# Front of a diffusion-step kernel: who sums the squares, when the roots are taken, and where the position rows and two coefficient pieces stand

## What is computed

```python
xs = x_sample + _grid_pos_embed(rows, GRID_W, D_MODEL)      # latent tokens, tiles 0 to 7; tile 8 is context
mod = silu(c) @ ada_w + ada_b                               # 1024 x 6144: shift, scale, gate, twice
h = x * rsqrt(mean(x * x) + eps) * norm1_g * (1 + sc1) + sh1
z = h @ w_in                                                # 1024 x 1280
```

## Time and profile before

| | |
|---|---|
| median of 3 runs | 1289.15 us (1288.95 to 1290.19) |
| profiled execution, its own time | 1290.97 us |
| its span, first to last instruction | 1289.2 us |
| mean granted PE clock over the span | 0.971 |
| busy: PE, DVE, ACT, POOL | 94%, 66%, 40%, 42% |

### The profile page before, as it was taken

One profiled execution on the slowest core, in us unless ns is written; L12 is line 12 of the kernel. 1 busy time (PEld: TensorE's weight loads), 2 busy tenths in 40 slices (PEclk: granted clock), 3 DMA queues, 4 the chain that ended last, 5 costly groups with the idle time before them and its releaser, 6 DMA issues.

```text
span 1289.2 us, 21127 instructions
## 1 busy us (share of the span) xinstructions
PE 1207.0 (94%) x7402; PEld 1057.2 (82%) x7402; DVE 854.6 (66%) x1329; ACT 513.7 (40%) x915; POOL 540.4 (42%) x375
## 2 busy tenths in 40 slices
PE   6879899975899998999999999999999999999996
PEld 2469788965457888899999999999889999999995
DVE  6459599899744266776677676677855555555558
ACT  3673711254255557433333334333332344243223
POOL 3589444662331005453554444554423333333330
PEclk9889999988899999999999999999899999999998
DMA  8915355878932425656666666765676777777781
GB/s 309 383 51 169 93 176 163 104 168 217 382 139 98 131 75 210 222 200 209 240 231 213 212 207 200 245 231 208 205 252 243 256 268 268 251 246 262 251 279 72
DMA packets 189649, 268.65 MB, mean 208 GB/s; under 512 B 14046, under 2 KB 108552, under 8 KB 186904
## 3 DMA queue, kind: packets, MB, share of 16 engines
q1 hardware_dynamic: 188128, 262.67, 62.0%
q0 software_dynamic: 1280, 4.72, 0.9%
q10 hardware_dynamic: 184, 0.55, 0.2%
HBM read 186.62 MB, written 81.26 MB: 208 GB/s over the span
## 4 chain that ended last, share of the span: by engine, by line
PE 78%; POOL 7%; issue 3%; DVE 3%; DMA 3%; ACT 3%; SPq 2%; DVEq 0%; POOLq 0%; ACTq 0%
PE banks L934 23%; PE banks L936 22%; PE banks L935 22%; PE banks L1213 3%; DMA ad<-in_ada_w 2%; PE banks L970 1%; PE banks L1093 1%; POOL wct L750 1%; POOL wct L748 1%; POOL sst L863 1%; PE banks L1110 1%; POOL wct L743 1%; PE banks L1116 1%; POOL wct_tmp L746 1%; POOL wct_tmp L744 1%
## 5 line engine op out<-in xcount | busy, mean ns | idle before, releaser
L886 POOL TENSOR_TENSOR raw13r<-raw13s,w13h 128x512 fp32r<-128x512 f32 x110 | 155.0, 1418 | 467.3 <-ACT w13h L1710 443.9
L935 PE MATMUL banks<-ntr,w13h 128*128 128x256 f32 (+1 forms) x1144 | 337.2, 295 | 0.0
L934 PE MATMUL banks<-ntr,w13h 128*128 128x256 f32 (+1 forms) x968 | 283.7, 293 | 3.2 <-POOL raw13r L886 2.1
L935 PEld LDWEIGHTS banks<-ntr,w13h 128*128 128x128 f32 x1144 | 216.5, 189 | 0.9
L934 PEld LDWEIGHTS banks<-ntr,w13h 128*128 128x128 f32 x968 | 183.5, 190 | 5.4 <-issue 2.3
L934 PE MATMUL banks<-f2h,f_hi 128*128 128x512 f32 x396 | 156.6, 396 | 0.4 <-DVE acc L2419 0.4
L936 PE MATMUL banks<-f2h,f_lo 128*128 128x512 f32 x396 | 156.3, 395 | 0.0
L935 PE MATMUL banks<-f2l,f_hi 128*128 128x512 f32 x396 | 156.2, 395 | 0.0
L936 PE MATMUL banks<-ntr,raw13r 128*128 128x256 f32 (+1 forms) x528 | 153.7, 291 | 0.0
L2285 DVE TENSOR_TENSOR acc<-acc,banks 128x512 f32<-128x512 f32 x170 | 112.8, 683 | 39.0 <-PE banks L936 30.8
L890 POOL TENSOR_TENSOR f2l<-f2s,f2h 128x1024 fp32r<-128x1024 f32 x44 | 106.1, 2433 | 34.6 <-ACT f2h L1714 34.6
(11 more groups left out here) (328 smaller groups left out, 2527.0 us busy)
## 6 DMA issues: line engine op xcount, KB each, us to landing
raw13s<-in_ffn_w SPq DMA_DIRECT2D x66, 512.0 KB, 4.5
parts<-w13h SPq DMA_DIRECT2D x110, 256.0 KB, 2.5
w13h<-parts SPq DMA_DIRECT2D x110, 256.0 KB, 2.7
f2s<-in_ffn_w SPq DMA_DIRECT2D x44, 512.0 KB, 4.2
ad<-in_ada_w SPq DMA_DIRECT2D x20, 1024.0 KB, 10.6
parts<-wsumr SPq DMA_DIRECT2D x66, 256.0 KB, 2.6
wsumr<-parts SPq DMA_DIRECT2D x55, 256.0 KB, 4.9
parts<-raw13r SPq DMA_DIRECT2D x44, 256.0 KB, 2.9
```

The lines of the kernel that those rows point to most:

```text
L886: nc.gpsimd.tensor_tensor(w13_low(x, f), w13_low(x, f, F32), w13h[x][:, :, :].bitcast(F32), ALU.subtract).then_inc(sem("w13_lo"), 1)
L934: nc.tensor.matmul(out, hi_w, hi_x, start=start, stop=False)
L935: nc.tensor.matmul(out, hi_w, lo_x, start=False, stop=False)
```

## The change

Tile sums 5 to 8 move from ACT to DVE, as `tensor_tensor_reduce` with an accumulator output; the product itself is thrown into the place where the scaled tile will stand later. DVE makes sum 5 after the last step of group 0, then the position adds 6 and 7, the inverse of group 1, sums 6, 7 and 8, and the inverse of group 2. ACT takes group 2's root behind the second step of group 1. PE makes position row 2 behind the raw transposes, rows 3, 4 and 5 in front of the modulation tiles 3, 4 and 5 instead of behind them, and rows 6 and 7 behind block 0 instead of inside it, in other banks. POOL makes coefficient piece 1 directly behind piece 0, issues the transfers of both behind the column halves 3 to 5, and makes the low part of weight tile 1 behind the column halves 6 and 7.

```diff
+    POS_BANK = (5, 6, 7, 5, 6, 7, 7, 6)
+    POS_PRIOR = (None, None, None, 0, 1, 2, 5, 4)
+    SQ_ACT = 5
...
         wc_piece(0)
+        wc_piece(1)
         w_low(0)
         for i in range(3, 6):
             pos_add(i)
-        w_low(1)
+        pool.wait_ge(sem("gsc"), 1)
+        wc_out(0)
+        wc_out(1)
         pos_add(6)
         pos_add(7)
-        pool.wait_ge(sem("gsc"), 1)
-        wc_out(0)
+        w_low(1)
         x_scale(3)
-        wc_piece(1)
-        wc_out(1)
         for i in range(6, 9):
             x_scale(i)
...
             if i >= 3:
-                pe.wait_ge(sem("pos_half"), i - 2)
-            mm(B[5 + i % 3][:, :], row_sel[:, i, :], pos_r[:, :], start=True, stop=True).then_inc(sem("pos_bank"), 1)
+                pe.wait_ge(sem("pos_half"), POS_PRIOR[i] + 1)
+            mm(B[POS_BANK[i]][:, :], row_sel[:, i, :], pos_r[:, :], start=True, stop=True).then_inc(sem("pos_bank"), 1)
...
-        for i in range(3):
-            pos_row(i)
+        pos_row(0)
+        pos_row(1)
         raws_turn()
+        pos_row(2)
         pe.wait_ge(sem("polar"), 2)
-        for k in range(KT - 1):
-            ada_tiles(0, k, k + 1, B[4])
-            if k in (3, 4, 5):
-                pos_row(k)
+        ada_tiles(0, 0, 3, B[4])
+        pos_row(3)
+        ada_tiles(0, 3, 4, B[4])
+        pos_row(4)
+        ada_tiles(0, 4, 5, B[4])
+        pos_row(5)
+        ada_tiles(0, 5, 7, B[4])
         x_turns(0, 2)
...
             if s == 1:
-                pe.wait_ge(sem("pos_half"), 8)
+                pe.wait_ge(sem("pos_half"), 4)
...
-        z_with_turns(0, {1: 6, 3: 7})
+        z_with_turns(0)
+        pos_row(6)
+        pos_row(7)
         z_block(1)
...
-        for i in range(3, 6):
+        for i in range(3, 5):
             square_sum(i)
         root(1)
         z_out(0)
-        for n in range(KT, KT + 4):
+        for n in range(KT, KT + 2):
             h_out(n)
+        root(2)
+        act.sem_inc(sem("squares"), NT - SQ_ACT)
         z_out(1)
-        for n in range(KT + 4, 16):
+        for n in range(KT + 2, 16):
             h_out(n)
-        for i in range(6, 9):
-            square_sum(i)
-        root(2)
         w_high(2)
...
-            dve.wait_ge(sem("squares"), i1)
+            dve.wait_ge(sem("squares"), min(i1, SQ_ACT))
...
+        def square_sum(i):
+
+            if i < 8:
+                dve.wait_ge(sem("pos_half"), i + 1)
+                dve.wait_ge(sem("pos_cols"), i + 1)
+            else:
+                dve.wait_ge(sem("x8_in"), 16)
+            x = xt[i][:, :].rearrange("p (k n) -> p k n", n=P)
+            step(nc.vector.tensor_tensor_reduce(x_scaled(i), x, x, 1.0, 0.0, ALU.mult, ALU.add, accum_out=ss[:, i:i + 1]))
...
-            if n in (1, 3, 5, 7):
+            if n in (1, 3):
                 pos_add(4 + n // 2)
             if n == KT - 1:
+                square_sum(5)
+                pos_add(6)
+                pos_add(7)
                 dve.wait_ge(sem("pos_half"), 8)
                 inverse_ms(1)
+                for i in range(6, 9):
+                    square_sum(i)
+                inverse_ms(2)
             if n == 2 * KT - 1:
-                inverse_ms(2)
                 w_low(2)
```

More of the change, by code:

```diff
@@ L1032, in _, with z_with_turns @@
         x_turns(2, 3)
-        def z_with_turns(s, pos=()):
+        def z_with_turns(s):
             i, b = ZSEQ[s]
@@ L1046, in z_with_turns @@
                     x_turns(KT * b + k + 3, KT * b + k + 4)
-                if k in pos:
-                    pos_row(pos[k])
                 pe.wait_ge(sem("h_split"), KT * b + k + 1)
@@ L1952, in pos_add @@
             dve.wait_ge(sem(f"x{i}_in"), 16)
-            TT(xt[i][:, 0:512], xt[i][:, 0:512], B[5 + i % 3][:, :], ALU.add).then_inc(sem("pos_half"), 1)
+            TT(xt[i][:, 0:512], xt[i][:, 0:512], B[POS_BANK[i]][:, :], ALU.add).then_inc(sem("pos_half"), 1)
         def inverse_ms(g):
```

## The result

The changed kernel takes 1282.01 us (median of 5, 1278.08 to 1282.40) beside 1289.15 us: ratio 0.9933, interval 0.9915 to 0.9951. The forecast was 1285.9; the gain is 7.1 us where 3.3 were forecast, beyond the forecast's own range (1284.2 to 1287.7), inside the wide one (1281.0 to 1290.5), and at the time of the rival "L1978 gets its turn after one POOL operation" (1282.2). The profiled execution took 1278.08 us with a span of 1276.3, the shortest of the five, so its trace shows more gain than the median. Lines have moved: L1977 and L1978 of before are now L1993 and L1994, DVE's low parts L2000, the sums L1977. (L1993 is a subtraction in the code; this text goes on calling the two the first and the second addition.)

The account below looks back on a forecast made before the run. Two PE holes, before group 2's transposes and before `state_inputs`, were taken to hang on group 2's root. Group 2 -0.6 and the second hole -2.7 gave -3.3 from 1289.15: 1285.9 us; own range 1284.2 to 1287.7, wide 1281.0 to 1290.5.

Parts of the forecast that it names:

- L1978 gets its turn after one POOL operation: Rival, DVE's second addition near 34 us: it waits for one POOL operation, not a whole piece; 1282.2 us, chance 0.2.
- forecast -2.7: PE's hole before `state_inputs` at 140 us closes because pieces 2 to 7 start earlier: -2.7 us.
- the rival of half rate: Rival, accumulating sums on DVE: they run at half throughput, 1.3 us more each; 1289.4 us, chance 0.13.
- piece 1 is ready meanwhile, takes the port at 34.05 and, as at 101.36, keeps it to 41.6: DVE/POOL port at 34 us: POOL's piece holds up DVE's second addition to about 42.6; +2.6 us on group 0.
- 39.99 + 2.6: Start of group 0's first transposes: 39.99 us before the change, delayed 2.6 us by the held second addition.
- -0.6 for group 2's first split: DVE's first split of group 2, behind low part 2: 83.3 instead of 83.85, so -0.6 us for all behind it.
- the 7.11 us: Earlier trace, DVE's low part at 101.36: it lasted past four POOL operation boundaries, taken as waiting for a whole piece.
- forecast to 83.3: End of low part 2 on DVE, because piece 2 was to hold the port from 74.7 to 82.2.
- little reached PE: DVE's low part at 101.36 meeting the pieces: it cost 6 us of DVE; low parts 3 and 4 given one us either way.
- as the rival had it: Rival, group 1: the granted clock falls while PE waits from 66 to 70 us; 1292 us, chance 0.1.
- the shift passes to the end: Behind 140 us each stage reads what this one makes, so a shift there reaches the end in full.
- Rows at -1.2: Position rows 6 and 7 leaving block 0, where ACT waited 1.19 us at 54.74: -1.2 us.

Follow-up runs that it names:

- e3: Changed kernel with sums 5 to 8 and the roots back as before, on ACT; 1288.55 us, ratio 0.9991.
- e15: The kernel of e10 run once more (sums, early root and POOL wait alone); 1287.63 us, ratio 0.9978.
- e8: Changed kernel with POOL making low part 1 ahead of the four transfers and column halves 6 and 7; 1281.40 us, ratio 0.9942.
- e1: Changed kernel with DVE waiting for its own first addition before issuing the second; 1280.88 us, ratio 0.9938.
- e11: The changed kernel run once more, unaltered, for one profile; 1280.26 us (one execution).
- e9: The kernel of e5 with low part 2 also waiting for the fifth operation of piece 2; 1283.44 us, ratio 0.9954.
- e5: Changed kernel with DVE's second addition made to wait for the fifth operation of piece 1; 1284.02 us, ratio 0.9954.
- e2: Changed kernel with POOL's old order: piece 1 behind the scaling of tile 3, no early piece; 1286.07 us, ratio 0.9976.
- e6: The kernel of e2 with POOL waiting for its own four scalings in front of piece 2; 1282.02 us, ratio 0.9947.
- e10: Kernel before the change with only the sums, group 2's early root and POOL's wait before piece 2; 1287.28 us, ratio 0.9970.
- e14: The kernel of e10 with position rows 6 and 7, their banks and adds moved behind block 0; 1284.12 us, ratio 0.9964.
- e4: Changed kernel with the position rows in their old places and banks; 1280.94 us, ratio 0.9932.
- e13: The kernel of e4 with POOL waiting for its own four scalings before piece 2; 1279.63 us, ratio 0.9932.

## Why the prediction missed

**Right.** With the sums on DVE and group 2's root early, both holes close: 5.30 us at 82 us, 2.67 us at 140 us (forecast -2.7); without them (e3) both are there, 5.29 and 2.54 us. The second hangs on the pieces too: in e15, with the root early and piece 1 late, it is still 2.61 us. The sums cost 1.23 + 0.08 = 1.31 us each where they do not meet POOL, below the 1.5 taken; the rival of half rate (2.6 us and more) did not happen. The Trainium skill (Vector Engine (DVE) Microarchitecture Reference, Points that are easy to get wrong) has half throughput for an instruction that it calls S2S2D2_STT, with two non-bf16 SBUF sources; that would be, by an estimate, twice the 1.285 us of the earlier trace rows. The trace agrees with no halving here, 1.23 us, but it records the sums as CUSTOM_DVE_ANT_0, and no run shows whether the rule is meant for that form. Low part 1's later place cost nothing that e8 could show.

**The step that failed** is "piece 1 is ready meanwhile, takes the port at 34.05 and, as at 101.36, keeps it to 41.6". In the changed kernel's trace DVE went first; where POOL did (e1, e8, e11), DVE had its turn one operation later. The addition was over between 34.84 and 36.34 and not at 42.6, and group 0 waited for PE's own work alone: it started at 37.88, in e11 at 39.81, where 39.99 + 2.6 was forecast. The forecast's -0.6 for group 2's first split (83.85 to 83.3) became -6.02 (77.83; -4.71 in e11, 79.14); in the first trace another 1.1 us were won between it and the first `state_inputs` (135.77 before, 128.66 now), and with the hole of 2.67 this makes 9.8 of the landmark's 9.97; the medians show 7.1.

The step was taken from one row, the 7.11 us. The same trace had another, for DVE's low part of weight tile 2, which began while POOL was in its three scalings:

```profile
76.38 1.94 DVE L1984 TENSOR_TENSOR w_lo<-wst,w_hi 128x1024 fp32r<-128x1024 f32 x1 [1.35 <-ACT w_hi L1434]
```

It had the port behind the first scaling and was over at 78.32, while the second took 2.87 us instead of 1.89. So the trace before already showed DVE getting its turn between POOL operations that follow at once, and the 7.11 us were one of two outcomes. The rival with a turn after one operation had price and mechanism; it was given 0.2 on the strength of one row against another. That its 1282.2 is so near the median is partly luck: it had low part 2 held by a piece and about 4 us for group 2, where low part 2 took 1.65 us and group 2 gained 6.0 (4.7 in e11).

**Low parts 2 and 3.** Low part 2 was mis-sized by the same assumption: forecast to 83.3, it was over at 73.50. What that was worth is open: forced behind piece 2 (e9) it adds nothing measurable to e5, but where it was held without the early piece (e2) PE stood 4.79 us. Low part 3, of whose 6 us "little reached PE", did cost PE 1.06 us before, by the PE timeline:

```profile
115.82 1.09 PE L1076 MATMUL banks<-ident,wb 128*128 128x128 f32 x8 [1.06 <-DVE wb L2049]
```

In the changed kernel it costs nothing (the wait of 0.34 us at the same place, 108.76, is ended by ACT), and 2.4 to 2.5 us where group 2 is early and the hold stays (e6, e10, e14, e15).

**What the hold explains.** With it forced, 1.4 to 2.0 of the miss of 3.9 us come back by the medians, 2.7 of 5.4 by the ratios: about a third to a half. The cause of the rest stays open; low part 3 and the clock from 45 to 62.5 us are candidates that the runs do not separate.

**The other rivals.** The clock stayed at 1.00 from 62.5 to 82 us in the changed kernel's first trace, but not in its second. e11's windows:

```profile
65.00:67.50 2.50, 1.96 (x7) 1.87 (x8) 2.16 (x5) 2.37 (x4) 2.50 (x2) 0.58 0.03 7
67.50:70.00 2.50, 2.50 (x15) 2.37 (x14) 1.58 (x3) 1.59 (x3) 2.50 (x2) 0.74 0.00 0
```

So the clock did fall in group 1 there (0.58 and 0.74, then 1.00 again), as the rival had it, but briefly: group 2's transposes started 1.31 us later than in the first trace (77.70), the landmark 1.32, and the run still took 1280.26 us, not 1292. That the shift passes to the end held.

**Rows at -1.2** were right as a place (ACT's wait) but not as a price of its own: nothing beside the early piece (e4, e13), and without it 1.8 to 3.5 us for rows 6 and 7 (e14), 3.0 to 5.3 for all (e6).

## What to carry to other kernels

Where two engines hold each other up at a port, do not price a meeting by one long row: look at who is stretched in every meeting, and force the wait in a run to price it. A wait of an engine for its own last operation, set where the other engine's operation is due, is a cheap way to hand the port over (in e6 POOL paused 0.08 us, and PE's wait of 4.79 us was gone). And parts of a change that only move work earlier are not additive: the early piece was worth 6 to 8 us without the rows and 2.3 to 2.6 with them, the rows 3.0 to 5.3 without the piece and nothing measurable with it.

## What was not expected of the hardware

**A wait at the port was one operation or the whole run.** Over these 17 traces, from 30 to 120 us, a sum, a low part or one of the two additions on DVE was still waiting when a POOL operation ended 100 times. In 57 of them no operation of POOL on tiles followed at once (a pause, in four cases the issue of a transfer), and DVE had the port each time. In 43 POOL's next was already up: in 25 DVE had the port all the same, at that first boundary; in the other 18 it missed this one and every further one, 57 boundaries in all and up to 8 in a row, until POOL paused, and then ended some 1.1 us later. None got in at a second or third boundary without a pause. What decides the first boundary stays open. The 11 that had begun to wait 0.42 us or less before it all missed it; of the 32 that had waited 0.56 us or more, 25 got in and 7 missed, one of these after 1.26 us (e2). The low part of tile 2 got in at it in each kernel with the early piece in which it met one, and in none of those with the sums and without the piece. The Trainium skill (SBUF, Who interferes with whom) calls the port an exclusive lock; the 25 agree with one operation as its length, the 18 do not.

**The granted clock moved between executions of one program.** From 45 to 62.5 us it was 0.80 in the changed kernel's first trace and 0.90 in e11's, from 62.5 to 76.4 us 1.00 and 0.88; and the first position row in block 0 took 2.07 us in e10 and 1.12 in e15, the same program.
